# Adaptive-norm gate slabs moved out of sample attention, and the hand-over to the output projection reordered

## The reference

```python
mod = silu(c) @ w_ada + b_ada                       # w_ada: 2048 x 12288
shift1, scale1, gate1, shift2, scale2, gate2 = split(mod, 6)
h  = rmsnorm(x, norm1_g) * (1 + scale1) + shift1
qa, ka, va, qb, kb, vb, r, log_a = project(h, w_in) # mixer A: attention, mixer B: GLA
oa = rmsnorm(mix_a(qa, ka, va), a_out_g)            # per head of 64
ob = rmsnorm(mix_b(qb, kb, vb, log_a), gla_out_g) * silu(r)
x  = x + gate1 * (concat(oa, ob) @ w_out)
h2 = rmsnorm(x, norm2_g) * (1 + scale2) + shift2
y, new_hist = conv_ffn(h2, conv_hist, w_up, conv_w, conv_b, w_down)
x  = x + gate2 * y                                  # gate2 is first used here
```

## Time and profile before

| | us |
|---|---|
| median of 3 runs | 1705.04 (1704.69 to 1705.55) |
| the profiled execution, its own time | 1704.05 |
| its span in the profile | 1702.5 |
| PE busy | 1633.8 (96%) |
| DVE busy | 893.8 (52%) |
| ACT busy | 718.6 (42%) |
| mean granted TensorE clock | 0.987 of full |
| HBM read | 361.45 MB |

### The profile page before, as it was taken

One profiled execution on the slowest core, in us unless ns is written; L12 is line 12 of the kernel. 1 busy time (PEld: TensorE's weight loads), 2 busy tenths in 40 slices (PEclk: granted clock), 3 DMA queues, 4 the chain that ended last, 5 costly groups with the idle time before them and its releaser, 6 DMA issues.

```text
span 1702.5 us, 29334 instructions
## 1 busy us (share of the span) xinstructions
PE 1633.8 (96%) x12210; PEld 1457.8 (86%) x12210; DVE 893.8 (52%) x1563; ACT 718.6 (42%) x1018; POOL 77.0 (5%) x134
## 2 busy tenths in 40 slices
PE   7799999999999888899899999999999999999997
PEld 3478888888887644699799999999999999999996
DVE  2445455555665534554744555455455556666563
ACT  2233354455555533533633333343343345555452
POOL 2000000001111000000000000000000000000000
PEclk9899999999999999999999999999999999999999
DMA  9998777789777899684845454544544545555550
GB/s 339 364 366 298 248 236 269 248 273 306 236 248 236 307 347 366 209 293 136 297 150 171 154 173 153 175 150 158 182 160 151 174 152 171 181 156 171 167 184 15
DMA packets 276001, 373.19 MB, mean 219 GB/s; under 512 B 8049, under 2 KB 192723, under 8 KB 275449
## 3 DMA queue, kind: packets, MB, share of 16 engines
q1 hardware_dynamic: 232272, 279.62, 49.3%
q10 hardware_dynamic: 35922, 71.38, 12.2%
q0 software_dynamic: 7680, 20.36, 3.4%
HBM read 361.45 MB, written 11.97 MB: 219 GB/s over the span
## 4 chain that ended last, share of the span: by engine, by line
PE 88%; DVE 4%; DMA 3%; ACT 2%; issue 1%; SPq 1%; ACTq 0%; POOL 0%; DVEq 0%; POOLq 0%
PE ps L889 24%; PE ps L890 23%; PE ps L891 23%; PE ps L840 5%; PE ps L1133 2%; DMA ring<-in_w_ada 2%; PE ps L1148 1%; PE ps L847 1%; DVE wlo L1906 1%; PE ps L1178 1%; ACT whi L1401 1%; DMA ring<-in_w_in 1%; PE ps L805 1%; DMA proj<-in_x_sample 1%; PE ps L1065 0%
## 5 line engine op out<-in xcount | busy, mean ns | idle before, releaser
L889 PE MATMUL ps<-hhi,whi 128*128 128x288 f32 x3136 | 943.3, 301 | 11.1 <-DVE hlo L1873 5.1
L891 PE MATMUL ps<-hhi,wlo 128*128 128x288 f32 x3136 | 926.8, 296 | 0.0
L890 PE MATMUL ps<-hlo,whi 128*128 128x288 f32 x3136 | 926.6, 295 | 0.0
L889 PEld LDWEIGHTS ps<-hhi,whi 128*128 128x128 f32 x3136 | 591.4, 189 | 55.4 <-issue 47.6
L890 PEld LDWEIGHTS ps<-hlo,whi 128*128 128x128 f32 x3136 | 591.0, 188 | 0.9
L891 PEld LDWEIGHTS ps<-hhi,wlo 128*128 128x128 f32 x3136 | 591.3, 189 | 0.0
L1781 DVE TENSOR_TENSOR wlo<-ring,whi 128x1024 fp32r<-128x1024 f32 x178 | 212.2, 1222 | 91.8 <-ACT whi L1384 91.4
L1384 ACT ACTIVATE whi<-ring 128x1024 fp32r<-128x1024 f32 x178 | 184.5, 1057 | 161.8 <-PE ps L891 161.8
L1906 DVE TENSOR_TENSOR wlo<-ring,whi 128x1024 fp32r<-128x1024 f32 x96 | 117.4, 1224 | 142.9 <-ACT whi L1401 142.6
L1401 ACT ACTIVATE whi<-ring 128x1024 fp32r<-128x1024 f32 x96 | 100.9, 1053 | 143.4 <-PE ps L891 126.9
L2393 DVE TENSOR_TENSOR wlo<-ring,whi 128x1024 fp32r<-128x1024 f32 (+1 forms) x94 | 105.7, 1132 | 57.3 <-ACT whi L1710 57.3
(11 more groups left out here) (296 smaller groups left out, 1182.6 us busy)
## 6 DMA issues: line engine op xcount, KB each, us to landing
ring<-in_w_up SPq DMA_DIRECT2D x88, 1024.0 KB, 5.1
ring<-in_w_ada ACTq DMA_DIRECT2D x58, 1024.0 KB, 6.4
ring<-in_w_in SPq DMA_DIRECT2D x48, 1024.0 KB, 7.9
ring<-in_w_down SPq DMA_DIRECT2D x32, 1408.0 KB, 6.6
ring<-in_cache_k_win SPq DMA_DIRECT2D x16, 1024.0 KB, 10.7
ring<-in_w_out SPq DMA_DIRECT2D x16, 1024.0 KB, 6.0
proj<-in_w_ada SPq DMA_DIRECT2D x14, 1024.0 KB, 9.8
vals<-in_cache_v_win SPq DMA_DIRECT2D x12, 1024.0 KB, 9.6
```

The source lines that it names most:

```text
L889: mm(out, w_hi, x_hi, start=start, stop=False)
L890: mm(out, w_hi, x_lo, start=False, stop=False)
L891: return mm(out, w_lo, x_hi, start=False, stop=stop)
```

## The change

The diff, shortened (in full for what moves; the semaphores' step names follow it, `gla_hi` and `gla_lo` becoming `gla_hi0`, `gla_hi1`, `gla_lo0`, `gla_lo1`):

```diff
         def gate_home(q):
-            if 2 <= q < 6:
-                return False, 1 + 2 * (q % 2), SL_OUT // SLOTS * 16 + (q // 2) * 16 - 16
-            l = q + 1 if q < 2 else (q - 6) % 4
-            return True, l, 16 if q < 2 else 16 * ((q - 6) // 4 + (2 if l in (1, 2) else 1))
+            if q < 4:
+                return False, 1 + 2 * (q % 2), SL_OUT // SLOTS * 16 + (q // 2) * 16
+            return True, q % 4, 16 * (q // 4)
...
 # SP
+            value_loads(NB // 2 - 1, 2)
+            last_value_loads()
+            sp.wait_ge(*ST.upto("k15", 3))
+            out_half(0)
+            out_half(1)
             gate_load(0)
             gate_load(1)
-            value_loads(NB // 2 - 1, 2)
-            sp.wait_ge(*ST.upto("k15", 3))
-            out_half(0)
-            last_value_loads()
-            out_half(1)
-            gate_load(2)
-            gate_load(3)
             for w in range(2, 6):
                 out_half(w)
...
                 if w < 12:
-                    gate_load(w - 2)
+                    gate_load(w - 4)
...
-            for q in range(10, 14):
+            for q in range(8, 12):
                 gate_load(q)
             half_loads(w_up, columns, CH_UP, range(4, 7))
+            gate_load(12)
+            gate_load(13)
+            half_loads(w_up, columns, CH_UP, range(7, 8))
+            columns = [512, D_FF + 512, 768, D_FF + 768]
+            half_loads(w_up, columns, CH_UP + 16, range(2))
             gate_load(14)
             gate_load(15)
-            half_loads(w_up, columns, CH_UP, range(7, 8))
-            half_loads(w_up, [512, D_FF + 512, 768, D_FF + 768], CH_UP + 16)
+            half_loads(w_up, columns, CH_UP + 16, range(2, 8))
...
 # PE
-            gate_slab(0)
-            gate_slab(1)
             probabilities(NB // 2 - 1)
             values(NB // 2 - 1)
             output(NB // 2 - 1)
-            gate_slab(2)
-            gate_slab(3)
...
-                if m == 0:
-                    pe.wait_ge(*OV.upto("gla_lo"))
+                if m < 2:
+                    pe.wait_ge(*OV.upto(f"gla_lo{m}"))
...
-            head_sums(0)
             for m in range(32):
-                if m == 2:
-                    pe.wait_ge(*BS.upto(*late("rows", 12)))
-                out_product(m)
-                if m == 0:
-                    head_sums(1)
-                if m == 7:
-                    late_turn(12)
                 if m == 4:
                     pe.wait_ge(*OV.upto("ms1"))
+                    gate_slab(0)
+                    gate_slab(1)
+                out_product(m)
+                if m < 2:
+                    head_sums(m)
...
-            for q in range(4, 7):
+            for q in range(2, 5):
                 gate_slab(q)
             norm2_sum(7)
-            for q in range(7, 10):
+            for q in range(5, 8):
                 gate_slab(q)
...
 # ACT
             act.wait_ge(*RG.upto("o", 3))
-            f(hhi[:, 8:16, :], proj[:, 40:48, :], ACT.Copy).then_inc(*OA.step("gla_hi"))
+            f(hhi[:, 8:12, :], proj[:, 40:44, :], ACT.Copy).then_inc(*OA.step("gla_hi0"))
             hi_of(out_slab, CH_OUT, 0)
             act.wait_ge(*SV.upto("out", 3))
             for n in range(2):
                 f(proj[:, 8 + 4 * n:12 + 4 * n, :], proj[:, 4 * n:4 * n + 4, :], ACT.Square)...
-            late_rows(12)
-            for j in range(1, 4):
+                if n == 0:
+                    f(hhi[:, 12:16, :], proj[:, 44:48, :], ACT.Copy).then_inc(*OA.step("gla_hi1"))
+                    hi_of(out_slab, CH_OUT, 1)
+            for j in range(2, 4):
                 hi_of(out_slab, CH_OUT, j)
...
 # DVE
-            dve.wait_ge(*OA.upto("gla_hi"))
-            v.tensor_tensor(hlo[:, 8:16, :], proj[:, 40:48, :], hhi[:, 8:16, :].bitcast(F32),
-                            ALU.subtract).then_inc(*OV.step("gla_lo"))
-            lo_of(out_slab, CH_OUT, 0)
+            for n in range(2):
+                t = slice(8 + 4 * n, 12 + 4 * n)
+                dve.wait_ge(*OA.upto(f"gla_hi{n}"))
+                v.tensor_tensor(hlo[:, t, :], proj[:, 40 + 4 * n:44 + 4 * n, :], hhi[:, t, :].bitcast(F32),
+                                ALU.subtract).then_inc(*OV.step(f"gla_lo{n}"))
+                lo_of(out_slab, CH_OUT, n)
             head_means(0)
-            lo_of(out_slab, CH_OUT, 1)
             head_means(1)
```

More of the change, by code:

```diff
@@ L364, in build @@
         OT = st("onorm_tensor", "sums0", "sums1")
-        OA = st("onorm_scalar", "gla_hi", "sq0", "sq1", "ln0", "ln1", "rs0", "rs1", "hi0", "hi1")
-        OV = st("onorm_vector", "gla_lo", "ms0", "ms1", "done0", "done1", "lo0", "lo1")
+        OA = st("onorm_scalar", "gla_hi0", "sq0", "gla_hi1", "sq1", "ln0", "ln1", "rs0", "rs1", "hi0", "hi1")
+        OV = st("onorm_vector", "gla_lo0", "gla_lo1", "ms0", "ms1", "done0", "done1", "lo0", "lo1")
         UV = st("out_vector", *(x for n in range(4) for x in (f"s{n}", f"u{n}")))
@@ L555, in gate_load @@
                 if spare:
-                    if q >= 10:
+                    if q >= 8:
                         sp.wait_ge(raw_used, RAW_OUT + q - 3)
@@ L559, in gate_load @@
                 else:
-                    if q >= 4:
+                    if q >= 2:
                         sp.wait_ge(raw_used, RAW_OUT + q - 1)
@@ L631, in _ @@
                 key_loads(g + 1, (0, 2))
+            value_loads(NB // 2 - 1, 2)
[3 more added lines that the diff above has]
+            out_half(1)
             gate_load(0)
             gate_load(1)
-            value_loads(NB // 2 - 1, 2)
-            sp.wait_ge(*ST.upto("k15", 3))
-            out_half(0)
-            last_value_loads()
-            out_half(1)
-            gate_load(2)
-            gate_load(3)
             for w in range(2, 6):
                 out_half(w)
-            sp.wait_ge(*OV.upto("gla_lo"))
+            sp.wait_ge(*OV.upto("gla_lo1"))
             for w in range(6, 16):
                 if w < 12:
-                    gate_load(w - 2)
+                    gate_load(w - 4)
                 out_half(w)
@@ L746, in _ @@
             hist = a["state_conv"][0].rearrange("b r c -> (b r) c")
-            pool.wait_ge(*OV.upto("gla_lo"))
+            pool.wait_ge(*OV.upto("gla_lo1"))
             pool.dma_start(hrow[:, 0], hist[:, 0:512]).then_inc(hist_in[0], 16)
@@ L905, in gate_slab @@
             def gate_slab(q):
[L907 to L910, removed]
+                if q in (8, 12):
+                    pe.wait_ge(*BS.upto(*late("rows", 10 + q // 4)))
                 spare, at, landed = gate_home(q)
                 pe.wait_ge(gate_in[at] if spare else full[at], landed)
-                ada_slab((3, 5, 7, 7)[q // 4], q, gate_rows[:, at] if spare else slab(at, 4, 512))
+                ada_slab((5, 7)[q // 4 % 2], q, gate_rows[:, at] if spare else slab(at, 4, 512))
             def late_turn(G):
@@ L1268, in after @@
                 def after(c):
[L1269 to L1274, removed]
+                    if c == 3 and (i, u) in ((0, 0), (0, 1), (0, 3), (1, 1)):
+                        late_turn({(0, 0): 12, (0, 1): 13, (0, 3): 14, (1, 1): 15}[i, u])
+                    if c == 3 and (i == 0 and u < 3 or i == 1 and u == 0):
+                        gate_slab(8 + 6 * i + 2 * u)
+                        gate_slab(9 + 6 * i + 2 * u)
                 return after
@@ L1409, in late_rows @@
                     act.wait_ge(*AT.upto("turn_b", 3))
-                f(mrow[:, :], ps[:, 3 if G <= 12 else 5 if G == 13 else 7, :], ACT.Copy).then_inc(*BS.step(f"rows{G % 2}"))
+                f(mrow[:, :], ps[:, 3 if G < 12 else 5 + 2 * (G % 2), :], ACT.Copy).then_inc(*BS.step(f"rows{G % 2}"))
             def spent(i, chunks, j):
@@ L1645, in _ @@
             norm_root(1)
-            late_rows(13)
+            late_rows(12)
             for j in range(2):
@@ L1679, in up_turn @@
                 his(6, 8)
-                if i == 0:
-                    late_rows(14)
+                if i < 2:
+                    late_rows(13 + 2 * i)
                 silu(0)
@@ L1686, in up_turn @@
                 if i == 0:
-                    late_rows(15)
+                    late_rows(14)
                 silu(1)
@@ L2280, in _ @@
                     norm2_scaled(n)
-                if j == 13:
-                    late_mod(12)
             norm_mean(1, 4)
@@ L2351, in up_turn @@
                 if i == 0:
-                    late_mod(13)
+                    late_mod(12)
                 gate(0)
                 los(10, 14)
-                if i == 0:
-                    late_mod(14)
+                if i < 2:
+                    late_mod(13 + 2 * i)
                 conv(1)
@@ L2369, in up_turn @@
                 if i == 0:
-                    late_mod(15)
+                    late_mod(14)
             for i in range(11):
```

2 lines of the change are left out of this document (1 added, 1 removed).

## The result

| | before | changed |
|---|---|---|
| median, us | 1705.82 (1703.32 to 1708.78, 10 runs) | 1713.45 (1709.17 to 1717.58, 10 runs) |
| ratio to before | | 1.0046, 95% interval 1.0035 to 1.0056 |
| profiled execution, span | 1702.5 | 1711.2 |
| mean granted clock in it | 0.987 | 0.984 |

The changed kernel is slower by 7.6 us, by 6.0 to 9.6 us over the interval. The forecast was +5.7 us, inside the range (1706.4 to 1714.0), on its side and somewhat small. The runs of one kernel lie some 5 to 8 us apart, which the three runs known before did not show. The spread goes with the clock: of the changed kernel's runs the shortest, 1709.2 us, had a mean granted clock of 0.986, the two longest, 1717.4 and 1717.6 us, one of 0.981.

A forecast was written before the change was run, and what follows sets the result against it. PE was taken as the bound, busy 1633.8 of 1702.5 us. Chunk 4 starting 3.8 us later plus 1.9 for two slabs gave +5.7 on 1704.05, and with 1.0 for the median 1710.7 us; range 1706.4 to 1714.0.

The forecast's parts named there:

- Last values first: Attention's last value products: PE's true wait for values is 0.2 us, not the weight load's 1.77; gain 0.2 us.
- The softmax hole: PE's idle time before the last probabilities grows from 2.05 to 3.9 us without slabs 0 and 1; its end stays.
- The rival in which the clock comes back in time: Longer softmax hole moves the first clock fall earlier, values run in 4.5 us; +1.6 us, 1706.6; chance 0.12.
- Two slabs in front of a full PE: Behind the start of chunk 4, 14 gate slabs stand instead of 12; cost +1.9 us.
- The hand-over's places: PE idles 3.5 us before chunk 0, about 2.5 us before chunk 2; slabs 0 and 1 cover chunk 4's wait.
- The clock: At chunk 0, behind 3.5 us of unbroken idle time, PE falls to 1.2 GHz and runs partly at half clock; 1.5 us.
- c: Clock cost at chunk 0: 1.5 us, the middle between no fall (0) and all of chunk 0 at half (3.25).
- a rival with chance 0.15: More cold time: chunk 0 wholly and sums 0 partly at half clock, or a late weight slab; +8 us, 1713; chance 0.15.
- The later stages: Up-projection's first two turns: slabs and loads keep their distance; cost 0, up to 2 us if a weight slab came late.

The follow-up runs named there:

- values_first: The kernel before with one part of the change alone: SP issues the last values ahead of the slab of w_out; ratio 1.0004 to before.
- changed_again: The changed kernel unaltered, run again beside before; median 1712.13 us, ratio 1.0047 to before.
- slabs_in_hole: The changed kernel with gate slabs 0 and 1 back in the softmax hole, 2 and 3 between head sums 1 and chunk 2; ratio 1.0018 to before.
- lower_part_first: The changed kernel with one swap on DVE: chunk 2's lower part ahead of the second head mean; ratio 1.0019 to before.
- filler: The changed kernel with six float32 matmuls of unused result ahead of chunk 0; median 1708.82 us, ratio 1.0017 to before.
- slabs_behind_sums: Before with slabs 2 and 3 moved behind head sums 1, the GLA half split in two, last values loaded first; ratio 0.9997 to before.
- single repair: The changed kernel with either unused matmuls ahead of chunk 0 (ratio 1.0017 to before) or chunk 2's lower part ahead of the second head mean (1.0019).
- both_repairs: The changed kernel with unused matmuls ahead of chunk 0 and chunk 2's lower part ahead of the second head mean; ratio 1.0033 to before.
- best_all_fillers: best_one_filler with four more unused matmuls in attention's last group, three in the softmax hole, one before the values; median 1699.49 us, ratio 0.9966 to before.
- best_one_filler: slabs_behind_sums with four float32 matmuls of unused result ahead of head sums 0; median 1703.91 us, ratio 0.9989 to before.
- before_fillers: The kernel before with four unused matmuls in attention's last group alone; median 1703.43 us, ratio 0.9990 to before.
- best_up_filler: best_all_fillers with six more unused matmuls at the start of the up-projection; median 1700.42 us, ratio 0.9973 to before.

## Why the prediction was right, and where it was small

**Last values first.** Right. The 1.77 us of the weight load was not PE's wait; values_first measures nothing. What I had not seen is the other side: the value products at half clock were slow enough to hide the transfer.

**The softmax hole.** Right: 3.77 us idle where 3.9 was expected, the value records 7.2 us as before. The rival in which the clock comes back in time fell: in neither profile of the changed kernel did the values run in under 7 us. That PE can run them in 4.5 was shown only by keeping it busy.

**Two slabs in front of a full PE.** The term was +1.9. From chunk 4 on the profile has +2.8 (3.7 - 0.9), of which 1.9 are the slabs; changed_again has +4.3. The rest, 0.9 and 2.4 us, lies where the up-projection starts and the clock falls a second time. The sum had nothing for it.

**The hand-over's places.** Right, each within 0.1 us: idle ahead of chunk 0 3.54 (3.5), ahead of chunk 2 2.58 (2.5), slabs 0 and 1 ahead of chunk 4 without a wait. Where the clock fell least, in changed_again, chunk 4 starts 36.1 us behind the first value product: +3.7, as the sum's +3.8.

**The clock.** This is the term that was mis-sized: c was put at 1.5 us, the middle of 0 and 3.25. In the two profiles of the changed kernel chunk 0 lost 5.9 - 3.25 = 2.65 and 4.54 - 3.25 = 1.3 us, and in slabs_in_hole and lower_part_first, with the same 3.54 us of idle time ahead of it, 2.5 and 2.65 us. In the first profile chunks 2 and 3 lost 1.6 more after the new wait. That second fall was in the prediction only as part of a rival with chance 0.15, though the wait that leads to it was in the sum. Together 4.3 us in the one, 1.3 in the other. So the forecast was close partly by luck: it left out the second fall, which one of the two executions has, and the extra one in the up-projection (0.9 and 2.4 us). The filler experiment shows that it is the clock: six matmuls that compute nothing made the kernel faster. The rule of the Trainium skill that I weighed ("TensorE: Matmul & The Clock Gate", "HAM oscillation — how this bites in real kernels"), that waits between groups of matmuls slow the next group, agrees with the trace at chunk 0 (all four profiles with 3.54 us ahead of it) and at chunk 2 in two of three profiles with 2.58 us. The rows of 688 to 695.8 us of before, where it stayed up, were the wrong ones to compare with: with slabs 2 and 3 moved away from there, in slabs_behind_sums, the clock fell.

**The later stages.** Right: PE waits for no weight slab in the first or second turn; its waits behind chunk 4 are all for DVE's parts of the second norm, 5.8 us in three, against 5.1 in four before.

**What stays open.** Each single repair gave back 4 to 5 us in the medians, while its place accounts for 2.1 to 2.5 against the first profile of the changed kernel, and for nothing against the second, whose chunk 4 lies at 36.1. Counted from the first value product to the end, the profiles keep the order that the places give: above before stand the two of the changed kernel by 9.3 and 8.0 us, the single repairs by 6.4 and 6.5, both together by 5.0. The rest goes with the clock. Over all runs, the mean granted clock against that of before in the same rounds is 0.0022 lower in changed_again, 0.0002 lower in lower_part_first, 0.0012 higher in filler and 0.0007 lower in both_repairs. Among the runs of one kernel 0.001 goes with some 1.2 to 1.5 us in most cases, so these differences stand for about +3, 0, -2 and +1 us (an estimate). From changed_again to filler that is some 5 us of clock, where chunk 0 had only 1.3 to 2.65 us to give, so the clock differed elsewhere too. It does so in code that is the same: from 590 to 600 us the granted clock was 0.83 in both profiles of the changed kernel and full in before. Whether a repair changes this or chance does, one profile per kernel can't show.

## What to carry to other kernels

Work moved out of an idle stretch of the bound engine costs its own length where that engine is full, and the gap that it leaves may cost as much again: behind 2.5 to 3.8 us without matmuls PE mostly ran at 1.2 GHz for the next 3 to 7 us here, though not every time. Before emptying such a gap, ask what fills it, and if nothing useful does, a few matmuls with an unused result are worth a trial. And before a transfer is moved forward, look whether its consumer really waits or only its weight load does; the answer can change when the consumer gets faster.

## What the runs showed of the hardware that I had not expected

- Filling gaps with unused float32 matmuls of 288 columns (0.52 us each at full clock, best_all_fillers and best_one_filler) shortened 40 value records from 7.31 to 4.50 us and head sums 0 from 3.87 to 2.10 us.
- Executions of one program on one core spread by 5 to 8 us (1703.3 to 1708.8 before, 1709.2 to 1717.6 changed). The two profiles of the changed kernel have the same waits to 0.01 us ahead of chunks 0 and 2, and differ in how much of the work behind them ran at half clock. The mean granted clock tells long runs from short ones: 0.986 at 1709.2 us, 0.981 at 1717.6 us.
- The same gap need not have the same effect. A fall followed 2.5 us ahead of head sums 0 in slabs_behind_sums, and 2.6 us ahead of chunk 2 in two of three profiles. It followed 2.2 us ahead of chunk 4 in both_repairs, not in lower_part_first. It followed 3.3 us at the up-projection in before, not in before_fillers (granted clock 1.00 from 818 to 826 us). The three gaps of 0.7 to 1.5 us with turns and a slab between them, before, were not followed by one; two of 0.7 and 1.0 us were in best_up_filler, not in best_all_fillers.
